# Heads of two mixers made token by token, normed along the free axis, then turned by transposes

## The chip, the cores and the metric

One core of one Trainium2 chip runs the whole program. The time is that of one execution on the device, in microseconds; the median of several executions is taken. The engines are named as in the profile: PE (TensorE), DVE (VectorE), ACT (ScalarE), POOL (GpSimd), SP (SyncE, which issues the transfers).

## What is computed

Two layers of an encoder trunk on 512 tokens of width 1024, all in fp32. The change lies in the first half of a layer, the mixer, where the outputs of eight heads of 128 channels are normed over their channels:

```python
def rms_norm(x, g):
    xf = x.astype(jnp.float32)
    y = xf * lax.rsqrt(jnp.mean(xf * xf, axis=-1, keepdims=True) + EPS)
    return (y * g.astype(jnp.float32)).astype(x.dtype)
...
    o = o.transpose(1, 0, 3, 2, 4).reshape(b, s, DA_HEADS, DA_V_DIM)
    o = rms_norm(o, out_g) * (1.0 - lam_init)
...
    o = rms_norm(o, out_g) * jax.nn.silu(g)
    return o.reshape(b, s, HG_WIDTH)
...
        x = x + jnp.concatenate([y_a, y_b.astype(y_a.dtype)], axis=-1) @ w_out[l]
        x = x + conv_glu_ffn(rms_norm(x, ffn_norm_g[l]), w_up[l], conv_w[l], conv_b[l], w_down[l])
```

The first norm is that of the four heads of differential attention (`dao` below), the second that of the four heads of a gated recurrence (`hgo`). Queries and keys of the attention (`dq`, `dk`) have a norm over 64 channels and a rotation of their own.

## The kernel before

**Tiles.** Activations lie transposed: 128 channels on the partitions, the 512 tokens along the free axis. A weight unit is 128 by 1024 values; for a product of fp32 accuracy it is split in a high and a low part (`wH`, `wL`), and each product is three matmuls of 512 columns (`triple`, L506 to L508). SP loads a unit, ACT makes the high part (`high_now`, L805), POOL the low part (`split`, L440, or `split_whole`, L446), and each has two buffers.

**Slots.** A layer's mixer is 40 slots. Slots 0 to 31 multiply one unit of `w_in` each (24 matmuls), slots 32 to 39 one of `w_out`. Between and behind the two halves of a slot's unit, each engine does its part of the recurrence (`item`, slots 7 to 30), of the attention (`scores`, `turn`, `values`, `row_max`, `combine`, `exponentials`, `back`, slots 17 to 33) and of the norms. There is no scheduler: each engine's order is the order of the code in its own loop over the slots, and an engine that waits holds up all that stands behind it on that engine.

**Norms of heads.** `STATS` says in which slot a norm's squares are summed: dq and dk in the slots 13, 14, 18, 19, 21, 22, 25, 26; the heads hgo0 in 20, hgo1 in 23, dao0 in 24, dao1 in 27, dao2 in 30, hgo2 in 31, hgo3 in 32, dao3 in 34. In such a slot ACT squares the head (`stat_square`), PE multiplies the squares with a constant matrix (`stat`, L546), which sums over the partitions and puts the sum in all of them; in the next slot ACT takes logarithm and exponential of 128x512 (`fin`, L839, L842) and DVE multiplies (`norm`, L1201; `rope` for dq and dk). For dao3 all of it is in slot 34. Then a hgo head is multiplied with its gate (`gating`, L1208), and each head is split in high and low (`high_out` on ACT, L939, `low_out` on DVE, L1215) for the product with `w_out`: heads 0 and 1 of `OUT_HEADS` in slot 31, 2 and 3 in slot 32, 4 and 5 in slot 33, 6 and 7 in slot 34, each pair wanted by PE one slot later.

**Bank 6.** One bank of PSUM takes turns: tokens of `hi` and `dv` (`to_tokens`), the attention's weights turned by four transposes (`turn`, L650), and the sums of `stat`. The order is a list (`bank6_uses`), and each use waits until ACT has read the one before.

Of the kernel before, what the change touches and what calls it, by code (L numbers as in the profile page):

```python
# [64 lines left out]
FINISH = {31: (0, 1), 32: (2, 3), 33: (4, 5), 34: (6, 7)}  # L65
LATE = 34

# [15 lines left out]
def bank6_uses():  # L83

    uses = []
    for s in range(SLOTS):
        if tokens_of(s) is not None:
            uses.append(("tokens", tokens_of(s)))
        if s == LATE:
            uses.append(("stat", STATS[s]))  # L90
        if step_of(s - 1) is not None:
            uses.append(("turn", step_of(s - 1)))
        if s in STATS and s != LATE:
            uses.append(("stat", STATS[s]))
    return {use: i for i, use in enumerate(uses)}
# [52 lines left out]
def build(nc, xT, wts, cst, msk, par, lbl, pos, outT):  # L148
# [14 lines left out]
    with ctx:  # L163
# [23 lines left out]
        sb("back", [P, 24])  # L187
# [55 lines left out]
        bank6_free = signal("bank6_free", B6)  # L243
        swapped = [signal(f"swapped{c}", 4 * 64) for c in range(2)]
        squared = signal("squared", 16)
        rstd_ln = signal("rstd_ln", 16)
        rstd_ready = signal("rstd_ready", 16)
        scaled = signal("scaled", 16)
        hg_q = signal("hg_q", 18)
# [17 lines left out]
        od_ready = signal("od_ready", HEADS)  # L267
# [111 lines left out]
        with nc.Block() as block:  # L379
# [122 lines left out]
            def _(pe):  # L502
                for l in range(DEPTH):
# [38 lines left out]
                    def stat(job):  # L542
# [3 lines left out]
                        pe.matmul(bank[6][:], cst_at(C_MEAN_H if job[0] in ("dk", "dq") else C_MEAN_D), sq[:, JOB[job] % 2, :],  # L546
                                  start=True, stop=True).then_inc(bank6_full.sem, 1)
# [70 lines left out]
                    def gather(pair):  # L618

                        pe.wait_ge(*hg_q.at(l, 9 * pair + 9))  # L620
                        for r in range(2):
                            hd = 2 * pair + r
                            pe.wait_ge(*st_ready.at(l, 4 * pair + 2 + r + 1))
                            for i in range(TT):
                                o = bank[2 + r][:, i * P:i * P + P]
                                pe.matmul(o, HI[:, i, hd * P:hd * P + P], A[:, r, i, :], start=True, stop=False)
                                if i > 0:
                                    m = pe.matmul(o, ST[:, r, 0, i - 1, :], head(QQ, 1, hd, i, 1), start=False, stop=i == TT - 1)
                                if i < TT - 1:
                                    m = pe.matmul(o, ST[:, r, 1, TT - 2 - i, :], head(QQ, 0, hd, i, 1), start=False, stop=True)  # L630
# [22 lines left out]
                    def values(a):  # L653
# [4 lines left out]
                        for k in range(TT):  # L658
                            m = pe.matmul(bank[7][:, qt * P:qt * P + P], V[:, k, hd * P:hd * P + P], wT[:, a % 2, k, :],  # L659
# [23 lines left out]
                    def out_half(u, half):  # L683
# [18 lines left out]
                        else:  # L702
                            if half == 0 and j < 6:
                                pe.wait_ge(*exps.at(l, STEPS))
                            elif half == 0:
                                pe.wait_ge(*((od_ready.at(l, HEADS)) if j == 6 else bank6_free.at(l, B6)))
# [8 lines left out]
                    for s in range(SLOTS):  # L715
# [8 lines left out]
                        if s == LATE:  # L724
                            stat(STATS[s])
# [6 lines left out]
                        if s in STATS and s != LATE:  # L732
                            stat(STATS[s])
                        if n is not None and n % PAIR_ITEMS == CARRY:
# [55 lines left out]
            def _(act):  # L790
# [7 lines left out]
                for l in range(DEPTH):  # L798
# [32 lines left out]
                    def fin(job):  # L831


                        j = JOB[job]
# [665 lines left out]
```

## Time and profile before

| | |
|---|---|
| median of three runs | 1429.94 us (1429.18 to 1429.96) |
| the profiled execution | 1427.0 us |
| its span | 1425.2 us |
| PE busy | 1388.1 us, 97% of the span |
| DVE, ACT, POOL busy | 846.8, 616.0, 711.5 us |
| chain that ended last | PE 78%, issue 7%, POOL 6%, DVE 4%, ACT 4% |
| POOL's split of a unit in one piece (L446) | 2412 ns |
| ACT's high part of a unit (L805) | 1057 ns |
| granted clock of PE | 0.997 of full speed |

A row of a timeline gives start and length in us, engine, line, operation, output and inputs, and in brackets how long the engine stood idle before it and what released it. A matmul's row is longer than the time that it holds up the next one, since matmuls overlap: the distance of two starts is the price.

### The profile page before, as it was taken

To read this page: it belongs to the slowest core of one execution; us is meant where nothing else is said; L and a number is where in the kernel's file an instruction comes from. 1 tells how busy PE (TensorE), PEld (TensorE's weight loads), DVE (VectorE), ACT (ScalarE), POOL (GpSimd) and SP (SyncE) were. 2 spreads that over 40 slices of the span, in tenths; PEclk is the share of its full clock that TensorE was granted. 3 is DMA by queue.
4 is the path that set the end of the run, shared out by engine and by line. 5 is a ranking of instruction groups with operands and counts; after the bars stand their busy time and mean duration, and the time that the engine had idled before them with its cause. 6 is when DMAs were issued, how large, how long until landed. Compare 5 with 4: busy or idle time off the path is not lost.

```text
span 1425.2 us, 18904 instructions
## 1 busy us (share of the span) xinstructions
PE 1388.1 (97%) x6556; PEld 1122.3 (79%) x6556; DVE 846.8 (59%) x1091; ACT 616.0 (43%) x878; POOL 711.5 (50%) x543
## 2 busy tenths in 40 slices
PE   5999999999999999999999999999999999999999
PEld 4887877777788888888878778777777888888887
DVE  6666698555676677600267767975557776675001
ACT  6343455374444444422343435554745444443211
POOL 2596376336444444444577853753374444444443
PEclk9999999999999999999999999999999999999999
DMA  4212122112232232223222221121132232232223
GB/s 152 89 60 92 57 60 75 60 45 89 89 103 88 88 103 91 101 92 103 88 89 75 67 91 52 58 74 45 61 103 76 101 101 90 88 103 94 98 98 108
DMA packets 36822, 121.07 MB, mean 85 GB/s; under 512 B 4897, under 2 KB 5409, under 8 KB 36769
## 3 DMA queue, kind: packets, MB, share of 16 engines
q1 hardware_dynamic: 36480, 119.64, 25.3%
q8 instruction: 33, 0.54, 0.2%
q10 hardware_dynamic: 288, 0.72, 0.1%
q14 instruction: 21, 0.16, 0.0%
HBM read 114.05 MB, written 2.10 MB: 81 GB/s over the span
## 4 chain that ended last, share of the span: by engine, by line
PE 78%; issue 7%; POOL 6%; DVE 4%; ACT 4%; DMA 0%; SPq 0%; POOLq 0%; DVEq 0%; ACTq 0%
PE bank L506 22%; PE bank L508 21%; PE bank L507 21%; PE bank L583 3%; POOL wL L446 3%; PE bank L641 2%; PE bank L659 2%; PE bank L546 2%; POOL rstd L370 1%; POOL wL L440 1%; ACT wH L805 1%; PE bank L650 1%; DVE QQ L1274 1%; DVE hL L358 1%; PE bank L614 1%
## 5 line engine op out<-in xcount | busy, mean ns | idle before, releaser
L446 POOL TENSOR_TENSOR wL<-raw,wH 128x1024 fp32r<-128x1024 f32 x142 | 342.6, 2412 | 419.7 <-ACT wH L813 357.3
L506 PE MATMUL bank<-hH,wH 128*128 128x512 f32 x1216 | 487.2, 401 | 25.4 <-POOL wL L440 11.7
L508 PE MATMUL bank<-hL,wH 128*128 128x512 f32 x1216 | 475.6, 391 | 0.0
L507 PE MATMUL bank<-hH,wL 128*128 128x512 f32 x1216 | 475.1, 391 | 0.0
L440 POOL TENSOR_TENSOR wL<-raw,wH 128x256 fp32r<-128x256 f32 x272 | 250.5, 952 | 196.3 <-ACT wH L805 196.3
L506 PEld LDWEIGHTS bank<-hH,wH 128*128 128x128 f32 x1216 | 229.2, 188 | 97.3 <-issue 40.9
L508 PEld LDWEIGHTS bank<-hL,wH 128*128 128x128 f32 x1216 | 229.1, 188 | 49.6
L507 PEld LDWEIGHTS bank<-hH,wL 128*128 128x128 f32 x1216 | 229.5, 189 | 44.9 <-issue 0.5
L813 ACT ACTIVATE wH<-raw 128x1024 fp32r<-128x1024 f32 x116 | 122.5, 1056 | 182.5 <-PE bank L508 179.8
L805 ACT ACTIVATE wH<-raw 128x1024 fp32r<-128x1024 f32 x95 | 100.4, 1057 | 150.0 <-PE bank L508 149.3
L506 PE MATMUL bank<-gH,wH 128*128 (+1 forms) x352 | 137.3, 390 | 0.2 <-issue 0.2
L507 PE MATMUL bank<-gH,wL 128*128 (+1 forms) x352 | 137.0, 389 | 0.0
L508 PE MATMUL bank<-gL,wH 128*128 (+1 forms) x352 | 137.0, 389 | 0.0
L1421 DVE TENSOR_TENSOR x<-x,bank 128x512 f32<-128x512 f32 x16 | 10.9, 683 | 199.8 <-PE bank L508 199.8
L1388 DVE TENSOR_TENSOR uu<-bank,rms 128x512 f32<-128x512 f32 x88 | 60.5, 691 | 92.4 <-PE bank L508 66.7
L1395 DVE SCALAR_TENSOR_TENSOR ua<-uu,cw,ua 128x511 f32<-128x511 f32 x44 | 114.4, 2601 | 1.5
L473 POOL TENSOR_TENSOR KK<-KK,T 128x512 f32<-128x512 f32 x56 | 71.6, 1300 | 30.1 <-PE bank L583 30.1
L506 PEld LDWEIGHTS bank<-gH,wH 128*128 128x128 f32 x352 | 66.1, 188 | 14.9 <-issue 0.9
L508 PEld LDWEIGHTS bank<-gL,wH 128*128 128x128 f32 x352 | 66.1, 188 | 13.8
L507 PEld LDWEIGHTS bank<-gH,wL 128*128 128x128 f32 x352 | 66.1, 188 | 13.5
L1031 ACT ACTIVATE ua<-ua 128x512 f32<-128x512 f32 x44 | 27.9, 633 | 94.2 <-DVE ua L1395 94.2
L1274 DVE TENSOR_TENSOR QQ<-QQ,T 128x512 f32<-128x512 f32 x56 | 66.7, 1230 | 0.0
(161 smaller groups left out, 1734.5 us busy)
## 6 DMA issues: line engine op xcount, KB each, us to landing
raw<-wts SPq DMA_DIRECT2D x211, 512.0 KB, 3.2
x<-xT SPq DMA_DIRECT2D x8, 256.0 KB, 5.5
swp<-K SPq DMA_DIRECT2D x32, 64.0 KB, 2.0
swp<-QO SPq DMA_DIRECT2D x32, 64.0 KB, 2.6
outT<-x SPq DMA_DIRECT2D x8, 256.0 KB, 2.0
raw<-wts ACTq DMA_DIRECT2D x1, 512.0 KB, 3.8
W<-pos SPq DMA_DIRECT2D x1, 256.0 KB, 6.9
R<-par SPq DMA_DIRECT2D x2, 109.0 KB, 3.4
```

The costliest lines, as they stand in the source:

```text
L440: m = pool.tensor_tensor(wL[:, s, at], raw[:, s, at], wH[:, s, at].bitcast(F32), ALU.subtract)
L446: pool.tensor_tensor(wL[:, s, :], raw[:, s, :], wH[:, s, :].bitcast(F32), ALU.subtract)\
L473: last = pool.tensor_tensor(v, v, w.to_broadcast([P, n, h]), ALU.mult)
L506: pe.matmul(out, wH[:, s, a:a + P], rhs_h, start=first, stop=False)
L507: pe.matmul(out, wL[:, s, a:a + P], rhs_h, start=False, stop=False)
L508: return pe.matmul(out, wH[:, s, a:a + P], rhs_l, start=False, stop=last)
L583: m = pe.matmul(o.rearrange("p (n two h) -> p n two h", two=2, h=h), kx[:, r, i * P:i * P + P], crossing(QQ, hd, i, h, 0), start=True, sto ...
L805: act.activation(wH[:, u % 2, :], raw[:, u % 2, :], ACT.Copy).then_inc(w_high.sem, 1)
L813: act.activation(wH[:, s, :], raw[:, s, :], ACT.Copy).then_inc(w_high.sem, 1)
L1274: last = dve.tensor_tensor(v, v, w[:, :, 1 - half, :].to_broadcast([P, S // h, h]), ALU.mult)
L1388: dve.tensor_tensor(uu[:, q, c, :], bank[2 * q + c][:], rms[:], ALU.mult).then_inc(up_ev.sem, 1)
L1395: dve.scalar_tensor_tensor(dst[:, q, 0:S - 1], uu[:, q, c, 1:S], w(2), dst[:, q, 0:S - 1], ALU.mult, ALU.add).then_inc(conv_done.sem, 1)
```

## The change

The products that make a head (`gather` for hgo, `values` for dao) swap their two operands, so that a head comes out with tokens on the partitions and channels along the free axis. ACT squares it as before. `stat` is gone for heads: DVE sums the squares along the free axis (`add_up`), ACT's `fin` works on 128x4, DVE's `norm` multiplies each token's row, four transposes on PE turn the head into bank 6 (`to_columns`), and ACT copies it out with the gain (`columns_out`). The transposes of a head stand at the end of the slot after the one in which its squares are taken, those of dao3 at the end of slot 34. For dao3, high and low part are made out of bank 6, in slot 35.

```diff
-FINISH = {31: (0, 1), 32: (2, 3), 33: (4, 5), 34: (6, 7)}
+FINISH = {31: (0, 1), 32: (2, 3), 33: (4, 5), 34: (6,), 35: (7,)}
...
+SCALED = {s if s == LATE else s + 1: job for s, job in STATS.items() if job[0] in OF_HEADS}
...
+                    def to_columns(job):
+
+                        pe.wait_ge(*scaled.at(l, JOB[job] + 1))
+                        bank6(("heads", job))
+                        for i in range(TT):
+                            m = pe.transpose(bank[6][:, i * P:i * P + P], out_head(*job)[:, i * P:i * P + P], cst_at(C_IDENT))
+                        m.then_inc(bank6_full.sem, 1)
...
-                                pe.matmul(o, HI[:, i, hd * P:hd * P + P], A[:, r, i, :], start=True, stop=False)
+                                pe.matmul(o, A[:, r, i, :], HI[:, i, hd * P:hd * P + P], start=True, stop=False)
...
-                            m = pe.matmul(bank[7][:, qt * P:qt * P + P], V[:, k, hd * P:hd * P + P], wT[:, a % 2, k, :],
+                            m = pe.matmul(bank[7][:, qt * P:qt * P + P], wT[:, a % 2, k, :], V[:, k, hd * P:hd * P + P],
...
-                        if s in STATS and s != LATE:
+                        if s in STATS and STATS[s][0] not in OF_HEADS:
                             stat(STATS[s])
+                        if s in SCALED:
+                            to_columns(SCALED[s])
...
+                        if job[0] in OF_HEADS:
+                            r = root_of[:, j % 2, :]
+                            act.wait_ge(*summed.at(l, TURNED[job] + 1))
+                            act.activation(r, sums[:, j % 2, :], ACT.Ln, bias=eps, scale=1.0 / P).then_inc(rstd_ln.sem, 1)
+                            act.wait_ge(*rstd_ln.at(l, TURNED[job] + 1))
+                            act.activation(r, r, ACT.Exp, scale=-0.5).then_inc(rstd_ready.sem, 1)
+                            return
...
+                    def columns_out(job):
...
+                        act.wait_ge(*bank6_full.at(l, BANK6[("heads", job)] + 1))
+                        gain = R[:, R_HGG:R_HGG + 1] if kind == "hgo" else dag[:, 0:1]
+                        act.activation(out_head(kind, hd), bank[6][:], ACT.Identity, scale=gain).then_inc(bank6_free.sem, 1)
...
+                        if OUT_HEADS[p] == LAST_HEAD:
+                            act.wait_ge(*bank6_full.at(l, BANK6[("heads", LAST_HEAD)] + 1))
+                            act.activation(yH[:, p, :], bank[6][:], ACT.Identity, scale=dag[:, 0:1]).then_inc(yH_ready.sem, 1)
+                            return
...
                         if s - 1 in STATS and s - 1 != LATE:
                             fin(STATS[s - 1])
+                        if s - 1 in SCALED and s - 1 != LATE:
+                            columns_out(SCALED[s - 1])
...
+                    def add_up(job):
+
+                        j = JOB[job]
+                        dve.wait_ge(*squared.at(l, j + 1))
+                        dve.tensor_reduce(sums[:, j % 2, :], sq[:, j % 2, :].rearrange("p (i c) -> p i c", i=TT), axis=AX.X, op=ALU.add)\
+                           .then_inc(summed.sem, 1)
...
-                        dve.scalar_tensor_tensor(o, o, gain, rstd[:, j % 2, :], ALU.mult, ALU.mult).then_inc(scaled.sem, 1)
+                        rows = root_of[:, j % 2, :].rearrange("p (i o) -> p i o", o=1).to_broadcast([P, TT, P])
+                        dve.tensor_tensor(o.rearrange("p (i c) -> p i c", i=TT), of.rearrange("p (i c) -> p i c", i=TT), rows, ALU.mult)\
+                           .then_inc(scaled.sem, 1)
...
                             row_max(step_of(s))
+                        if s in SCALED and s != LATE:
+                            norm(SCALED[s])
                         if n is not None:
                             grow(pair, lv)
```

In short: `summed` counts the sums, `fin` no longer reads bank 6 for a head, and `gating` and `high_out` wait for `columns_out` instead of the norm.

PE at the end of slot 21 (C is the identity or the constant matrix, QQ a hgo head, W and wT the attention's weights), before:

```order
L508 MATMUL bank<-hL,wH 128x512
L546 MATMUL bank<-sq,C 128x512 [waits bank6_free,squared]
L659 MATMUL bank<-wT,V 128x128 [waits bank6_free]
L659 MATMUL bank<-wT,V 128x128 x3
L583 MATMUL bank<-QQ,kx 128x128 [waits a_msk,kx_ready,hg_q]
```

and in the changed kernel:

```order
L553 MATMUL bank<-sq,C 128x512 [waits bank6_free,squared]
L561 MATMUL bank<-C,QQ 128x128 [waits bank6_free,scaled]
L561 MATMUL bank<-C,QQ 128x128 x3
L674 MATMUL bank<-V,wT 128x128 [waits bank6_free]
L674 MATMUL bank<-V,wT 128x128 x3
L598 MATMUL bank<-QQ,kx 128x128 [waits a_msk,kx_ready,hg_q]
```

The transposes of hgo0 stand directly behind the `stat` of dk2, which uses the same bank; slot 25 has the same pair with dao0 and dk3.

ACT in slots 32 and 33 (ACT_TABLE_LOAD and T belong to the gates' silu, yH is the high part of a head), before:

```order
L805 ACTIVATE wH<-raw 128x1024 [waits w_used,raw_in1]
L839 ACTIVATE rstd<-bank,C 128x512 [waits scaled,bank6_full]
L842 ACTIVATE rstd<-rstd 128x512 [waits bank6_free]
L859 ACTIVATE sq<-QQ 128x512 [waits oh_ready]
L939 ACTIVATE yH<-QO 128x512 [waits scaled]
L939 ACTIVATE yH<-QQ 128x512 [waits gated]
L916 ACTIVATE wT<-bank 128x512 [waits pv_mm,bank6_full]
```

and in the changed kernel:

```order
L820 ACTIVATE wH<-raw 128x1024 [waits w_used,raw_in1]
L855 ACTIVATE root_of<-sums,C 128x4 [waits summed,scaled]
L857 ACTIVATE root_of<-root_of 128x4 [waits rstd_ln]
L888 ACTIVATE QO<-bank,dag 128x512 [waits bank6_full]
L880 ACTIVATE sq<-QQ 128x512 [waits oh_ready]
L972 ACTIVATE yH<-QO 128x512 [waits bank6_free]
L972 ACTIVATE yH<-QQ 128x512 [waits gated]
L945 ACTIVATE wT<-bank 128x512 [waits pv_mm,bank6_full]
```

Two activations of 512 columns have become two of 4 columns and one of 512 that waits for PE's transposes and frees bank 6.

DVE in slot 21 (E and sm are the attention's, A the recurrence's), before:

```order
L1311 TENSOR_REDUCE sm<-bank 128x1 [waits sc_mm]
L1311 TENSOR_REDUCE sm<-bank 128x1
L1274 TENSOR_TENSOR QQ<-QQ,T 128x256x2 [waits tot_ready,hg_q,lv_mm]
L1274 TENSOR_TENSOR QQ<-QQ,T 128x256x2
L1201 SCALAR_TENSOR_TENSOR QQ<-QQ,R,rstd 128x512 [waits rstd_ready]
L1171 TENSOR_TENSOR QO<-bank,rms 128x512 [waits w_used]
```

and in the changed kernel:

```order
L1357 TENSOR_REDUCE sm<-bank 128x1 [waits sc_mm]
L1357 TENSOR_REDUCE sm<-bank 128x1
L1242 TENSOR_TENSOR QQ<-QQ,root_of 128x512 [waits rstd_ready]
L1320 TENSOR_TENSOR QQ<-QQ,T 128x256x2 [waits tot_ready,hg_q,lv_mm]
L1320 TENSOR_TENSOR QQ<-QQ,T 128x256x2
L1207 TENSOR_TENSOR QO<-bank,rms 128x512 [waits w_used]
```

The norm has moved ahead of `grow`; the sum along the free axis stands at the end of the slot before.

## Rows read from the trace of the kernel before

**Rows 1.** Page, part 1: busy us, share of span, instructions.

```profile
PE 1388.1 (97%) x6556; PEld 1122.3 (79%) x6556; DVE 846.8 (59%) x1091; ACT 616.0 (43%) x878; POOL 711.5 (50%) x543
```

**Rows 2.** Waits of PE, 130 to 350 us: us, times, longest.

```profile
PE bank L650 <- ACT rstd L839: 0.7, 1, 0.7
PE bank L506 <- POOL wL L446: 0.6, 2, 0.4
```

**Rows 3.** Timeline of PE, slots 22 to 27 of layer 0: start, length.

```profile
199.11 0.60 PE L650 MATMUL bank<-C,W 128*128 128x128 f32 x4
...
199.78 0.40 PE L507 MATMUL bank<-hH,wL 128*128 128x512 f32 x1
...
202.32 1.02 PE L546 MATMUL bank<-sq,C 128*128 128x512 f32 x2
203.18 1.05 PE L659 MATMUL bank<-wT,V 128*128 128x128 f32 x8
...
236.24 1.05 PE L659 MATMUL bank<-wT,V 128*128 128x128 f32 x8
...
247.89 0.82 PE L599 MATMUL bank<-C,KK 128*128 128x128 f32 x6
248.64 1.13 PE L641 MATMUL bank<-K,QO 64*128 64x512 f32 x4
```

**Rows 4.** Timeline of PE, slot 21 of layer 0.

```profile
188.37 0.60 PE L650 MATMUL bank<-C,W 128*128 128x128 f32 x4
...
191.56 1.02 PE L546 MATMUL bank<-sq,C 128*128 128x512 f32 x2
```

**Rows 5.** Timeline of ACT, end of slot 21, starts of 22 and 26.

```profile
190.51 0.68 ACT L924 ACTIVATE E<-bank,sm 128x512 f32<-128x512 f32 x1
...
191.84 1.06 ACT L805 ACTIVATE wH<-raw 128x1024 fp32r<-128x1024 f32 x1
192.78 0.69 ACT L839 ACTIVATE rstd<-bank,C 128x512 f32<-128x512 f32 x1
...
236.60 0.67 ACT L839 ACTIVATE rstd<-bank,C 128x512 f32<-128x512 f32 x1
```

**Rows 6.** Timeline of DVE, slot 21 and slot 28.

```profile
185.54 0.98 DVE L1322 SCALAR_TENSOR_TENSOR W<-E,sm 128x512 f32<-128x512 f32 x1
...
190.65 1.23 DVE L1201 SCALAR_TENSOR_TENSOR QQ<-QQ,R,rstd 128x512 f32<-128x512 f32 x1
...
261.04 0.74 DVE L1201 SCALAR_TENSOR_TENSOR QO<-QO,dag,rstd 128x512 f32<-128x512 f32 x1
```

**Rows 7.** Timeline of ACT, slots 31 to 33.

```profile
295.92 0.60 ACT L916 ACTIVATE wT<-bank 128x512 f32<-128x512 f32 x1 [2.29 <-PE bank L650]
...
305.39 0.62 ACT L939 ACTIVATE yH<-QQ 128x512 fp32r<-128x512 f32 x1
...
312.05 0.67 ACT L839 ACTIVATE rstd<-bank,C 128x512 f32<-128x512 f32 x1
```

**Rows 8.** Timeline of PE, slot 33 of layer 0, then of layer 1.

```profile
312.77 0.65 PE L650 MATMUL bank<-C,W 128*128 128x128 f32 x4 [0.67 <-ACT rstd L839]
...
316.02 1.05 PE L659 MATMUL bank<-wT,V 128*128 128x128 f32 x8
...
1017.53 0.66 PE L650 MATMUL bank<-C,W 128*128 128x128 f32 x4 [0.67 <-ACT rstd L839]
```

**Rows 9.** Groups by line and form: busy us, mean ns, idle before.

```profile
L1311 DVE TENSOR_REDUCE sm<-bank 128x1 f32<-128x512 f32 x64 | 41.1, 683 | 10.1 <-PE bank L641 9.9
...
L650 PE MATMUL bank<-C,W 128*128 128x128 f32 x128 | 19.2, 272 | 1.3 <-ACT rstd L839 1.3
...
L971 ACT ACTIVATE sm<-sm 128x16 f32<-128x16 f32 x1 | 0.2, 198 | 0.0
```

**Rows 10.** Timeline of DVE, slot 32 of layer 0.

```profile
302.71 0.68 DVE L1208 TENSOR_TENSOR QQ<-QQ,T 128x512 f32<-128x512 f32 x1
...
305.52 1.14 DVE L1215 TENSOR_TENSOR yL<-QO,yH 128x512 fp32r<-128x512 f32 x1 [2.13 <-ACT yH L939]
```

More of the change, by code:

```diff
@@ L64 @@
 OUT_HEADS = [("dao", 0), ("dao", 1), ("dao", 2), ("hgo", 0), ("hgo", 1), ("hgo", 2), ("hgo", 3), ("dao", 3)]
-FINISH = {31: (0, 1), 32: (2, 3), 33: (4, 5), 34: (6, 7)}
+FINISH = {31: (0, 1), 32: (2, 3), 33: (4, 5), 34: (6,), 35: (7,)}
 LATE = 34
+OF_HEADS = ("hgo", "dao")
+LAST_HEAD = ("dao", HEADS - 1)
+SCALED = {s if s == LATE else s + 1: job for s, job in STATS.items() if job[0] in OF_HEADS}
+TURNED = {job: j for j, job in enumerate(SCALED.values())}
 def item_of(s):
@@ L186, in build @@
         R = sb("R", [P, NR])
-        sb("back", [P, 24])
+        sums = sb("sums", [P, 2, TT])
+        root_of = sb("root_of", [P, 2, TT])
+        sb("back", [P, 8])
         bank = [ctx.enter_context(nc.psum_tensor(f"bank{i}", [P, S], F32)) for i in range(8)]
@@ L545, in stat @@
                         bank6(("stat", job))
-                        pe.matmul(bank[6][:], cst_at(C_MEAN_H if job[0] in ("dk", "dq") else C_MEAN_D), sq[:, JOB[job] % 2, :],
-                                  start=True, stop=True).then_inc(bank6_full.sem, 1)
+                        pe.matmul(bank[6][:], cst_at(C_MEAN_H), sq[:, JOB[job] % 2, :], start=True, stop=True)\
+                          .then_inc(bank6_full.sem, 1)
+                    def to_columns(job):
[4 more added lines that the diff above has]
+                        m.then_inc(bank6_full.sem, 1)
                     def item(n):
@@ L1357, in _ @@
                             prep(s // 18)
+                        if s == LATE:
+                            add_up(STATS[s])
+                            norm(STATS[s])
                         for p in FINISH.get(s, ()):
-                            if s != LATE or p < KT - 1:
-                                low_out(p)
-                        job = STATS[LATE] if s == LATE else STATS.get(s - 1) if s - 1 != LATE else None
-                        if job in ROPES:
-                            rope(ROPES.index(job))
-                        elif job is not None:
-                            norm(job)
-                        if s == LATE:
-                            low_out(KT - 1)
+                            low_out(p)
+                        if STATS.get(s - 1) in ROPES:
+                            rope(ROPES.index(STATS[s - 1]))
+                        if s in STATS and s != LATE and STATS[s][0] in OF_HEADS:
+                            add_up(STATS[s])
                         if l == 0 and s in (2, 4, 5):
```

55 lines of the change are left out of this document (28 added, 27 removed).

## Prediction

> **What bounds the kernel now.** I read the page first: PE is busy 97% of the span, of the other engines DVE comes next with 59% [rows 1]. Then the waits of PE in the mixer stage of layer 0, where every line of the change lies: in 220 us PE waits 1.3 us in all, 0.7 of it before the transposes of `turn` in slot 33 [rows 2]. So an instruction added to PE or taken from it counts in full, except where PE already waits, and a new wait on PE counts in full. Then PE's timeline for prices, and the timelines of ACT and DVE for when things are ready. Layer 1 repeats layer 0's pattern (its idle time at slot 33 is the same 0.67 us [rows 8]), so I work out layer 0 and double.
>
> **What PE is rid of.** Per layer eight `stat` matmuls for the heads. One starts at 202.32 and the next instruction at 203.18 [rows 3]: 0.86 us. 8 x 0.86 = 6.88 us off.
>
> **What PE gets.** Per layer eight groups of four transposes (`to_columns`). No such group stands in the trace for heads, but `turn` is the same operation, 128x128 f32 against the identity. It starts at 199.11, and the second matmul behind it at 199.78, 0.67 later; two matmuls of the stream are 0.23 apart with no transposes ahead, so four transposes cost 0.44. Ahead of other f32 matmuls there are six transposes from 247.89 to 248.64, 0.125 each, which makes 0.50 for four [rows 3]. Most of the new groups stand before `values`, some before a stream. The bounds are 0.41 and 0.50; I take 0.43, nearest to the row with four: 8 x 0.43 = 3.44 us on.
>
> One transpose alone has a duration of 272 ns [rows 9], but the four of a group lie over one another and are over in 0.60 us [rows 3]. Were they in series, a group would take 4 x 0.272 = 1.09, dearer than the `stat` that it replaces; that is a rival below. The Trainium skill (TensorE: Matmul & The Clock Gate, "Part 4: PE-mode transpose") gives about 275 ns for a 128x128 transpose inside a kernel and says nothing of how a group overlaps; whoever prices a group by it gets 1.10 us. The trace agrees on the one and speaks against the sum.
>
> **Operands swapped.** `gather` and `values` change which side is stationary. Both sides are 128x128 f32 and the counts are equal: nothing, between -0.3 and +0.3 us per layer.
>
> **Two new waits on PE.** `to_columns` of a head stands one slot behind the place of its `stat`. In slots 21 and 25 that place also holds the `stat` of a rope job (dk2, dk3), which stays. Both use bank 6, so the transposes wait until ACT has read the `stat` result. ACT gets to that (L839) only after the high half of a weight unit (L805, 1.06 us), which itself waits for the same slot's last matmul. Slot 25: PE is free at 236.24 [rows 3], ACT's L839 starts at 236.60 and takes 0.67 [rows 5], so bank 6 is free at 237.27, and PE goes on some 0.05 later, as it does in slot 33 (312.05 + 0.67 = 312.72 against 312.77) [rows 7, 8]. The wait is 1.08 us. Slot 21: PE's `stat` starts at 191.56, ends its share at 192.42 by the 0.86 above [rows 4]; L839 runs from 192.78 to 193.47 [rows 5]: 1.1 us. But PE now reaches this point 0.86 earlier, and ACT is late there already: its last exponential starts at 190.51 and two of them with the reads take 1.45, so L805 follows at 191.84 without a gap [rows 5]. ACT's inputs in that slot come from PE as well, and most of ACT moves along; the part that hangs on DVE does not. I take 1.23. Behind the waiting transposes stand `values`, the next level of the recurrence and the next scores; all are delayed with it and nothing hides it, since PE is the bound. Together 2.31 us on, between 1.8 and 3.3.
>
> **DVE.** Per head it gets a sum along the free axis. The nearest row is the row maximum, 683 ns from PSUM [rows 9]; the norm by columns takes the place of one by a full tile, which took 0.74 to 1.23 us [rows 6]. So about 0.65 more per head. DVE is 59% busy, but in slots 20 to 22 it runs behind PE without idle time. There W of slot 21 is done at 185.54 + 0.98 = 186.52 and PE's transposes of it start at 188.37: 1.85 us of cover [rows 4, 6]. PE comes 0.86 earlier, DVE 0.65 later, which leaves 0.34. I count nothing. If the sum costs 1.23 (the dear duration of the norm row, as with POOL busy beside it), 0.24 us of wait appears and ACT's exponentials slip by up to 0.5, so up to 0.75 per layer. The norm now stands ahead of `grow` and the gating; `grow`'s result is first wanted when PE enters slot 22, after the new wait above, and is ready by then.
>
> **ACT in the slots 31 to 33.** Here ACT sets the time: it runs through from the copy at 295.92 (the last at which it waits for PE) to 312.72, where it frees bank 6 and PE, idle for 0.67, starts `turn` [rows 7, 8]. Whatever PE saves behind 295.92 and ahead of 312.77 is lost in this wait. That is two exchanges of a `stat` for four transposes (the ends of slots 31 and 32): 2 x 0.43 = 0.86 us given back. ACT's own work: `fin` on 128x4 instead of 128x512. A small activation (128x16) takes 198 ns [rows 9], two with the pass from one to the other some 0.45 (an estimate) against 1.24 (L839 and L842 as they follow each other). For it comes the copy out of bank 6 with a gain, 0.67 long by L839, which also reads bank 6 with an operand per partition [rows 5], 0.6 to the next start. Slot 32: 0.45 + 0.6 against 1.24, 0.2 earlier. But DVE now does the norm of hgo2 (which waits for this `fin`) ahead of the gating of hgo0, and ACT's L939 at 305.39 waits for that gating. Today it is done at 302.71 + 0.68 [rows 10]; now it comes after about 303.5 + 1.1 + 0.7 to 1.1, for POOL's split runs beside it and a tensor-tensor there took 1.14 [rows 10], so 305.3 to 305.8: ACT between 0.2 earlier and 0.4 late. Slot 33: `fin` plus the copy, 1.05 to its end, against the 0.67 of L839 alone: 0.35 later. In sum ACT frees bank 6 between 0.1 and 0.75 later; I take 0.5.
>
> **Slots 33 to 35, the last head.** Four transposes more at the end of slot 33, and in slot 34 a `stat` gone and four transposes come: counted above. `values` of the last step starts at 316.02 [rows 8] and ends 1.05 later; from there square, sum, two small activations, norm: about 3.5 us, and PE is in slot 34 for 24 matmuls of 0.23, 5.5 us. The transposes then do not wait. Behind them ACT and DVE split the head (0.7 + 0.7 us and the passes) under the 12 matmuls of slot 35's first half, 2.7 us: cover left 0.5 to 1 us. ACT's weight unit for slot 36 comes about 1 us later than now, with POOL's 2.4 us behind it, and is still 1 us early. I count nothing.
>
> **Sum per layer:** -6.88 + 3.44 + 2.31 + 0.86 + 0.50 = +0.23 us. Both layers: +0.5 us. The profiled execution took 1427.0 us, so 1427.5; the median of the runs shown is 2.9 higher at 1429.94, so I forecast **1430.4 us**. With all low ends (transposes 0.41, waits 1.8, ACT 0.1, operands -0.3) it is -1.1 per layer, 1427.7; with all high ends (0.50, 3.3, DVE's 0.24, ACT 0.75, +0.3) +2.6 per layer, 1435.1, which needs them all at once.
>
> **Rivals.**
> - *The new waits are short* (faster): the gain of 3.44 per layer stands, and slots 21 and 25 cost nearly nothing, because ACT frees bank 6 by the time `stat` is over. -3.44 + 0.86 + 0.5 = -2.1 per layer, 1425.7. Against it: ACT's weight copy can't start before the slot's last matmul and lies ahead of L839 in both slots [rows 5]. For it: only that nothing in the trace shows a group in this place. 0.11, with all mixtures that gain over 2.9 us.
> - *DVE's lag becomes PE's wait* (slower): the extra sum and the earlier norm push W, row maxima and exponentials of slots 20 to 24 past the point at which PE wants them. It decides once DVE slips more than 1.0 us per head there (1.85 less 0.86). At 1.2 us a head, with `fin` waiting for the sum, PE would wait in four slots for 0.3 to 0.5 each, +1.5 per layer on my sum: 1433.4. For it: DVE has no idle time in these slots. Against it: its idle time returns by slot 24. 0.08.
> - *Transposes in series* (slower): each of a group waits for the one before, as they might with other waits around them: 1.09 instead of 0.43 [rows 9]. 8 x 0.66 = 5.3 per layer on my sum, less some 0.9 that slot 33's idle time hides, 4.4: 1439. Against it: 0.60 for four [rows 3]. 0.02. The skill's page named above leads to the same time.
>
> **How the numbers follow.** The forecast's case has 0.79. What a measurement can tell from no change is 0.2%, 2.9 us: 1427.1 to 1432.8. The first rival lies below it, the other two above: 0.11, 0.79, 0.10. The range takes in the sum's ends as far as single ones reach and stops short of the rivals: 1427.6 to 1432.8.
>
> **What would show it.** In the profile after: PE busy about 3.4 us less per layer, and PE's waits up by about as much. Transposes of heads in slots 21 and 25 preceded by 1.0 to 1.3 us of idle time put down to ACT's L839, none at the other six heads. `turn` in slot 33 preceded by about 2 us of idle time, not 0.67. DVE rows of the sum near 0.65 us. The prediction is wrong if the heads' transposes cost more than 0.5 us a group, if PE waits for DVE anywhere in slots 20 to 24, or if idle time before the slot 21 and 25 groups is under half a microsecond.

## Result and the profile after

The changed kernel takes **1436.14 us** (median of 5 runs, 1434.73 to 1436.60); the kernel before takes 1429.31 beside it (5 runs, 1428.99 to 1429.96). The ratio of the means is 1.0044, 95% interval 1.0033 to 1.0055: slower by 0.44%. The forecast was 1430.4 with a range up to 1432.8. The profiled execution took 1434.73 us, span 1432.5. One of e8's eleven executions below was slow, 2319.67 us at a mean granted clock of 0.557, and is in no ratio; e8's median without it is 1425.16.

The page's part 1 of the kernel after, in the form of [rows 1]:

```profile
PE 1385.2 (97%) x6588; PEld 1122.8 (78%) x6588; DVE 860.5 (60%) x1107; ACT 612.4 (43%) x890; POOL 716.2 (50%) x543
```

PE's busy time falls by 2.9 us in two layers, less than the forecast 3.4 a layer, but this row can't be read as the saving. The row of a 128x512 matmul is 0.39 us long where the next one starts 0.23 later, so busy stretches overlap, and a wait that is new leaves such a tail uncovered. The saving is read from starts, below.

The waits of PE from 130 to 350 us of the kernel after (us, times, longest), where [rows 2] had two lines:

```profile
PE bank L561 <- ACT rstd L861: 2.2, 2, 1.2
PE bank L665 <- ACT QQ L888: 1.8, 1, 1.8
PE bank L665 <- DVE W L1368: 1.2, 1, 1.2
PE bank L561 <- ACT wT L945: 0.5, 1, 0.5
...
PE bank L665 <- ACT QO L888: 0.3, 1, 0.3
```

L561 is `to_columns`, L665 is `turn`. The first two lines were forecast (two bank-6 meetings, and a wait of about 2 us in slot 33). The lines on DVE's W, on ACT's wT and on ACT's QO were not. Where each stands is in PE's timeline of layer 0 (start, length, last the idle time and what ended it), the answer to [rows 3, 4, 8]:

```profile
190.67 0.63 PE L665 MATMUL bank<-C,W 128*128 128x128 f32 x4 [1.19 <-DVE W L1368]
...
193.90 1.02 PE L553 MATMUL bank<-sq,C 128*128 128x512 f32 x2
196.11 0.63 PE L561 MATMUL bank<-C,QQ 128*128 128x128 f32 x4 [1.19 <-ACT rstd L861]
196.57 1.06 PE L674 MATMUL bank<-V,wT 128*128 128x128 f32 x8
...
240.32 0.63 PE L561 MATMUL bank<-C,QO 128*128 128x128 f32 x4 [1.02 <-ACT rstd L861]
240.78 1.06 PE L674 MATMUL bank<-V,wT 128*128 128x128 f32 x8
...
301.78 0.60 PE L561 MATMUL bank<-C,QO 128*128 128x128 f32 x4
302.22 1.06 PE L674 MATMUL bank<-V,wT 128*128 128x128 f32 x8
...
307.55 0.66 PE L665 MATMUL bank<-C,W 128*128 128x128 f32 x4 [0.27 <-ACT QO L888]
...
316.86 0.66 PE L665 MATMUL bank<-C,W 128*128 128x128 f32 x4 [1.78 <-ACT QQ L888]
...
320.74 0.63 PE L561 MATMUL bank<-C,QQ 128*128 128x128 f32 x4 [0.47 <-ACT wT L945]
321.21 1.06 PE L674 MATMUL bank<-V,wT 128*128 128x128 f32 x8
```

**How far PE is behind, slot by slot.** I compare starts of the same instruction group in both traces. The transposes of W in slot 18, ahead of every norm of a head, start at 154.71 before and 156.33 after: +1.62 that has nothing to do with the edit (below, b1). Take that off, and PE's lag at `values` is: slot 20 -0.85, slot 21 +2.53, slot 24 +1.26, slot 25 +2.92, slot 31 +1.25, slot 33 +3.57 (321.21 against 316.02 [rows 8]), and +3.16 behind slot 34. Layer 1 gives +3.54 up to slot 33. The sum on record gives +0.66 up to slot 33 and +0.23 behind slot 34. So a layer lost 2.9 us more than forecast, two layers 5.9 us, which is the whole miss of 5.7 between the medians and the forecast.

The prices of the operations come out of the groups by line and form (busy us, mean ns, idle before), in the form of [rows 9]:

```profile
L1231 DVE TENSOR_REDUCE sums<-sq 128x4 f32<-128x512 f32 x16 | 10.8, 676 | 0.0
...
L1242 DVE TENSOR_TENSOR QQ<-QQ,root_of 128x512 f32<-128x512 f32 x8 | 6.7, 834 | 8.2 <-ACT root_of L857 8.2
...
L888 ACT ACTIVATE QQ<-bank,R 128x512 f32<-128x512 f32 x8 | 5.4, 676 | 0.3
```

The sum costs 0.68 (0.60 to the next start) and the copy out of bank 6 0.68. They are as priced, and so are the transposes: a group of four at 301.78 is followed by the next instruction at 302.22, 0.44 later.

### The profile page after: what moved, and what is told of

It reads as the page before. It is cut to its first block, busy times and chain, and to the rows that moved or that the text cites. A ratio compares the mean times of both kernels' runs of the same rounds, so it can differ in the third digit from the quotient of the medians.

```text
span 1432.5 us, 18994 instructions
## 1 busy us (share of the span) xinstructions
PE 1385.2 (97%) x6588; PEld 1122.8 (78%) x6588; DVE 860.5 (60%) x1107; ACT 612.4 (43%) x890; POOL 716.2 (50%) x543
## 4 chain that ended last, share of the span: by engine, by line
PE 78%; issue 6%; DVE 6%; POOL 5%; ACT 4%; DMA 0%; SPq 0%; POOLq 0%; DVEq 0%; ACTq 0%
PE bank L513 22%; PE bank L515 22%; PE bank L514 22%; PE bank L598 3%; POOL wL L453 2%; PE bank L656 2%; PE bank L674 2%; POOL rstd L377 1%; POOL wL L447 1%; DVE QQ L1320 1%; ACT wH L820 1%; DVE hL L365 1%; PE bank L629 1%; PE bank L665 1%; PE bank L553 1%
## 5 line engine op out<-in xcount | busy, mean ns | idle before, releaser
L447 POOL TENSOR_TENSOR wL<-raw,wH 128x256 fp32r<-128x256 f32 x272 | 255.1, 968 | 191.0 <-ACT wH L820 191.0
```

Of the source, the lines that this page charges most:

```text
L447: m = pool.tensor_tensor(wL[:, s, at], raw[:, s, at], wH[:, s, at].bitcast(F32), ALU.subtract)
```

## Experiments

All times stand beside runs of the kernel before on the same chip. "Lag per layer" is the shift against the first trace of the kernel before, from the first transposes of W (slot 18) to `values` of slot 33; both layers agree within 0.04 us in every kernel, and a repeat of the kernel before gives 0.00.

| kernel | median us (runs) | before | ratio of means, 95% interval | lag per layer, us |
|---|---|---|---|---|
| changed | 1436.14 (5) | 1429.31 | 1.0044, 1.0033 to 1.0055 | +3.57 |
| e1 columns apart | 1431.73 (11) | 1429.67 | 1.0010, 1.0001 to 1.0019 | +0.93 |
| e2 gating first | 1432.63 (10) | 1429.67 | 1.0018, 1.0009 to 1.0028 | +2.30 |
| e3 head 0 later | 1433.38 (11) | 1429.67 | 1.0021, 1.0012 to 1.0030 | +1.50 |
| e4 all three | 1424.89 (5) | 1429.67 | 0.9965, 0.9951 to 0.9978 | -0.99 |
| e5 before, one sum | 1429.23 (10) | 1429.15 | 0.9999, 0.9990 to 1.0009 | 0.00 |
| e6 before, two sums | 1431.91 (10) | 1429.15 | 1.0017, 1.0008 to 1.0027 | +0.87 |
| e7 columns first | 1425.15 (7) | 1429.15 | 0.9974, 0.9963 to 0.9985 | -0.89 |
| e8 turned W first | 1425.33 (11) | 1429.59 | 0.9973, 0.9964 to 0.9982 | -2.33 |
| e9 products ahead | 1435.12 (5) | 1429.59 | 1.0041, 1.0027 to 1.0054 | +3.51 |
| e10 best of all | 1424.28 (5) | 1429.59 | 0.9964, 0.9950 to 0.9977 | -3.06 |

The lag is free of one thing that the medians hold: each fall of PE's granted clock costs an execution 1.53 us (below, b1). The executions of the kernel before had a mean granted clock of 0.995 to 0.996, e4's 0.997 to 0.998, e7's 0.996 to 0.997, and all of e8's but the one named above 0.994 to 0.996. So differences of 1 to 2 us between medians can be the clock's; the argument goes by the lags.

### e1: the meetings on bank 6

```diff
+MOVED = {21: 23, 25: 27}
+COLUMNS = {MOVED.get(s, s): job for s, job in SCALED.items()}
...
-                        if s in SCALED:
-                            to_columns(SCALED[s])
+                        if s in COLUMNS:
+                            to_columns(COLUMNS[s])
```

(The order of uses of bank 6 and ACT's `columns_out` follow `COLUMNS` too.)

> The transposes of the recurrent head 0 go from slot 21 to 23 and those of the differential head 0 from slot 25 to 27, slots where no square product of a dk or dq stands right ahead of them; the norms stay where they are, so DVE's order is untouched. Theory 'three places': the changed kernel's saving is eaten by two meetings on bank 6 (1.19 and 1.02 us of idle time a layer), by DVE's lag in slot 21 (1.19) and by slots 31 to 33. Then the two ACT waits ahead of the transposes go (2.2 a layer), the wait of the turn in slot 21 for DVE stays at about 1.2, and the time is 1436.1 - 4.4 = 1431.7 (1431 to 1432.5). Rival 'DVE sets slots 21 to 25': the idle time only moves to the next turn, and the time stays within 1 us of 1436.1. Rival 'it is the start': 1.6 us of the loss lies ahead of slot 14 and comes again in every kernel that is built from the changed one.

Measured: 1431.73, the expected time. PE's waits, 130 to 350 us:

```profile
PE bank L667 <- ACT QQ L890: 1.8, 1, 1.8
PE bank L667 <- DVE W L1370: 1.2, 1, 1.2
...
PE bank L563 <- ACT wT L947: 0.5, 1, 0.5
PE bank L667 <- ACT QO L890: 0.3, 1, 0.3
```

The 2.2 us line is gone and the others haven't moved. A layer is 2.64 us shorter for 2.21 us of idle time: these waits of PE cost some 0.2 us each more than their rows say. The rival of a DVE that sets slots 21 to 25 falls: the wait for DVE stayed at one place and one size.

### e2: the gating ahead of the norm

```diff
+                        for p in FINISH.get(s, ()):
+                            if OUT_HEADS[p][0] == "hgo" and p != 5:
+                                gating(OUT_HEADS[p][1])
                         if s in SCALED and s != LATE:
                             norm(SCALED[s])
...
-                            if OUT_HEADS[p][0] == "hgo":
+                            if p == 5:
                                 gating(OUT_HEADS[p][1])
```

> DVE's gating of the recurrent heads 0, 1 and 3 goes ahead of the norm in the same slot; only head 2's stays behind it. Theory 'three places': in slot 33 the norm of head 3 waited 2.8 us for its root while the gating that ACT's copy and then ACT's copy of the turned W (and so bank 6) wait for stood behind it. With head 1's product ahead of the norm the wait of the last transposes in slot 33 for ACT (0.47 us) goes and the turn's wait there (1.78) may shrink: 0.5 to 1.0 us a layer, 1434.1 to 1435.1. Rival 'ACT sets slots 31 to 33 by its own work': the gating is early but ACT no earlier, within 0.4 us of 1436.1.

Measured: 1432.63, and 1.27 us a layer less than the changed kernel, more than expected. The changed kernel's DVE and then ACT in slot 33 show the chain that the edit cuts:

```profile
312.73 0.75 DVE L1368 SCALAR_TENSOR_TENSOR W<-E,sm 128x512 f32<-128x512 f32 x1
316.27 0.89 DVE L1242 TENSOR_TENSOR QQ<-QQ,root_of 128x512 f32<-128x512 f32 x1 [2.79 <-ACT root_of L857]
317.08 2.37 DVE L1250 TENSOR_TENSOR QQ<-QQ,T 128x512 f32<-128x512 f32 x2
```

```profile
318.33 0.63 ACT L972 ACTIVATE yH<-QQ 128x512 fp32r<-128x512 f32 x1 [1.52 <-DVE QQ L1250]
319.48 0.63 ACT L972 ACTIVATE yH<-QQ 128x512 fp32r<-128x512 f32 x1 [0.52 <-DVE QQ L1250]
320.02 0.58 ACT L945 ACTIVATE wT<-bank 128x512 f32<-128x512 f32 x1
```

DVE idles 2.79 us for the root of head 3. Behind the norm stand two gating products, ACT's two roundings wait for those (1.52 and 0.52), and behind the roundings stands ACT's copy of the turned W, the one that empties bank 6 for PE's last transposes. With the gating first, PE's 0.47 us wait is gone, and the turn's wait in slot 33 is 1.17 in place of 1.78.

### e3: slots 20 and 21 without a head

```diff
-STATS = {13: ("dk", 0), 14: ("dq", 0), 18: ("dk", 1), 19: ("dq", 1), 20: ("hgo", 0), 21: ("dk", 2), 22: ("dq", 2),
-         23: ("hgo", 1), 24: ("dao", 0), 25: ("dk", 3), 26: ("dq", 3), 27: ("dao", 1), 30: ("dao", 2),
+STATS = {13: ("dk", 0), 14: ("dq", 0), 18: ("dk", 1), 19: ("dq", 1), 21: ("dk", 2), 22: ("dq", 2),
+         23: ("hgo", 0), 24: ("dao", 0), 25: ("dk", 3), 26: ("dq", 3), 27: ("dao", 1), 28: ("hgo", 1), 30: ("dao", 2),
```

> The recurrent head 0 is squared, summed and scaled in slots 23 and 24 (in place of head 1's) and head 1 in slots 28 and 29; slots 20 and 21 have no head's work any more. Theory 'three places': both waits of slot 21 go, the turn's for DVE (1.19) and the transposes' for ACT (1.19), and with them DVE's slow small operations beside GpSimd; slot 25 keeps its 1.0. 2.4 us a layer, 1436.1 - 4.8 = 1431.3 (1430.5 to 1432.5). Rival 'only the bank': DVE's wait comes back in slots 21 to 24 in another place, and 1.2 a layer is gained, 1433.7. Rival 'the DVE lag is not the sum's': the turn in slot 21 waits for DVE as before by 1 us or more, although no sum stands ahead of it.

Measured: 1433.38, above the expected 1430.5 to 1432.5, and 2.07 us a layer less than the changed kernel. The transposes' wait in slot 21 is gone, but the one for DVE is only halved (0.54 us), though no sum stands ahead of it. DVE and then POOL in slot 21 of this kernel:

```profile
186.35 0.57 DVE L1364 TENSOR_TENSOR sm<-sm,lamc 128x1 f32<-128x1 f32 x1
186.95 1.51 DVE L1365 TENSOR_SCALAR E<-E,sm 128x512 f32<-128x512 f32 x1
188.50 1.68 DVE L1368 SCALAR_TENSOR_TENSOR W<-E,sm 128x512 f32<-128x512 f32 x1
```

```profile
185.72 1.19 POOL L474 TENSOR_TENSOR T<-T 128x256 f32<-128x256 f32 x2 [2.86 <-PE bank L598]
186.86 2.78 POOL L480 TENSOR_TENSOR KK<-KK,T 128x512 f32<-128x512 f32 x2
```

In the kernel before the same three DVE operations took 0.16, 0.92 and 0.98 us (W's row is in [rows 6]). DVE, then POOL of that stretch in the kernel before:

```profile
184.39 0.16 DVE L1318 TENSOR_TENSOR sm<-sm,lamc 128x1 f32<-128x1 f32 x1
184.59 0.92 DVE L1319 TENSOR_SCALAR E<-E,sm 128x512 f32<-128x512 f32 x1
```

```profile
184.61 1.37 POOL L467 TENSOR_TENSOR T<-T 128x256 f32<-128x256 f32 x2 [3.71 <-PE bank L583]
185.94 3.04 POOL L473 TENSOR_TENSOR KK<-KK,T 128x512 f32<-128x512 f32 x2
```

In e3 the first of the three ends at 186.92, where GpSimd's T is done (186.91). E ends at 188.46 and W at 190.18, 0.2 and 0.5 us behind the ends of KK's two products, which lie near 188.25 and at 189.64. GpSimd starts when PE's `item` ends. PE now comes 0.86 us earlier to it, since no `stat` stands at the end of slot 20, while DVE comes as before, so GpSimd's KK products stand beside DVE's E and W rather than its short T products.

The Trainium skill (SBUF — State Buffer, "Who interferes with whom") says that a DVE operation with two inputs in SBUF and a GpSimd operation that reads SBUF exclude each other, the later one standing still until the first is done. The end of the first agrees with that. W's agrees but for 0.2 us: it ends 0.5 behind KK, where its whole 0.75 (its length at 312.73, under e2) would be expected. The price of standing beside KK is W's 1.68 against the 0.98 of the kernel before. No run takes GpSimd's products out of the slot, so the exclusion is read from these ends and not tested by itself.

### e5 and e6: the cover measured in the kernel before

```diff
+                        if s == 20:
+                            for i in range(N):
+                                dve.tensor_reduce(spare[:, 4 * i:4 * i + 4],
+                                    cosT[:].rearrange("p (i c) -> p i c", i=TT), axis=AX.X, op=ALU.add)
```

Each sum is of 128x512, at the end of slot 20. N is 1 in e5 and 2 in e6. Nothing reads the sums.

> The kernel before, with one more sum of 128x512 along the free axis on DVE at the end of slot 20, of a table that nobody waits for; PE's work is untouched. W of slot 21 was done 1.85 us ahead of PE's transposes. Theory 'GpSimd doubles the lag': a DVE that is 0.6 later runs its two products under GpSimd's KK products, at 1.0 to 1.7 us each in place of 0.92 and 0.98; W ends 1.1 to 1.6 later, so that 0.3 to 0.7 of cover is left and PE doesn't wait. Rival 'plain cover': W ends 0.6 later, 1.25 left. Both: the time within 1 us of 1429.7.

> The same with two such sums, 1.2 us. Rival 'plain cover': 1.85 - 1.2 = 0.65 left, no wait of PE for W in slot 21, the time as before. Theory 'GpSimd doubles the lag': W ends 2.4 to 3.2 later, PE waits 0.5 to 1.3 us for it in slot 21, once a layer, +1.0 to +2.6 on the whole: 1430.7 to 1432.3.

Measured: e5 as before; e6 PE waits, once a layer, and a layer is 0.87 us longer. DVE in slot 21 of e6, then PE:

```profile
184.65 1.27 DVE L1368 TENSOR_REDUCE back<-cosT 128x4 f32<-128x512 f32 x2
...
186.62 0.24 DVE L1318 TENSOR_TENSOR sm<-sm,lamc 128x1 f32<-128x1 f32 x1
186.90 1.49 DVE L1319 TENSOR_SCALAR E<-E,sm 128x512 f32<-128x512 f32 x1
188.43 1.68 DVE L1322 SCALAR_TENSOR_TENSOR W<-E,sm 128x512 f32<-128x512 f32 x1
```

```profile
190.25 0.63 PE L650 MATMUL bank<-C,W 128*128 128x128 f32 x4 [0.67 <-DVE W L1322]
```

Plain cover would have left 1.85 - 1.19 = 0.66 us. The two sums cost 2.54: 1.19 themselves and 1.35 by which the three operations behind them ran longer. In e5 one sum cost 0.60 + 0.68 (0.26, 0.80 and 1.68 us in place of 0.16, 0.92 and 0.98), so 0.59 is left. The time of e6 is 2.8 us above before's, of which 1.7 is this; the rest may be the clock, which its trace shows fallen in both layers (below, b1).

The same account closes for every kernel of the slot. It says where the cover went; the reason for the longer operations is the one under e3. In it "sum ahead" counts 0.60 for each sum and -0.60 for W made ahead of the eviction, and "left" is the time by which W was done ahead of PE's arrival (worked out from starts and lengths as above):

| kernel | PE earlier | sum ahead | three operations longer | 1.85 less these | left, measured |
|---|---|---|---|---|---|
| before, one sum (e5) | 0 | 0.60 | 0.68 | +0.57 | +0.59 |
| before, two sums (e6) | 0 | 1.19 | 1.35 | -0.69 | -0.69 |
| head 0 later (e3) | 0.86 | 0 | 1.70 | -0.71 | -0.71 |
| changed | 0.86 | 0.60 | 1.79 | -1.40 | -1.39 |
| products ahead (e9) | 0.86 | 0 | 1.70 | -0.71 | -0.71 |
| best of all (e10) | 0.86 | -0.60 | 1.00 | +0.59 | +0.58 |

### e9: the four operations for W ahead of the eviction

```diff
+                        if s == 21:
+                            combine(step_of(s - 1))
                         if 0 < s <= N_IN:
                             evict(s - 1)
...
-                        if step_of(s - 1) is not None:
+                        if step_of(s - 1) is not None and s != 21:
                             combine(step_of(s - 1))
```

> The changed kernel with one edit: in slot 21 DVE makes W (combine) ahead of the eviction of the unit's bank, so its four operations for W start 0.6 us earlier, about where they stood before the change. Theory 'GpSimd doubles the lag': the sum's 0.60 us is undone, and so is most of the 1.8 us by which these operations ran longer beside GpSimd's products: PE's wait for W in slot 21 goes from 1.19 us to 0 to 0.3, and 0.9 to 1.5 us a layer come out: 1436.1 - 2.4 = 1433.7 (1433 to 1434.5). Rival 'plain lag': only the 0.6 us is undone, the wait is 0.6: 1434.9. Rival 'the bank takes it': the square product at the slot's end comes earlier but ACT's square, behind the later eviction, does not, and PE waits there or before the transposes for what it gained: 1436.

Measured: 1435.12, above the expected 1433 to 1434.5; lag per layer 3.51 against 3.57. "GpSimd doubles the lag" is too strong here: starting 0.6 us earlier did not bring the operations out from beside KK (1.70 longer, as in e3), so only the sum was undone and the wait for W is 0.54, as "plain lag" has it. And even that was lost, as the third theory has it. PE's timeline of slot 21 in e9:

```profile
188.54 0.63 PE L665 MATMUL bank<-C,W 128*128 128x128 f32 x4 [0.54 <-DVE W L1368]
...
194.60 0.63 PE L561 MATMUL bank<-C,QQ 128*128 128x128 f32 x4 [1.83 <-ACT rstd L861]
```

ACT reads bank 6 (L861) behind its exponentials of the slot, and these wait for DVE's row maxima, which stand behind W and the eviction. In e9 W is earlier and the eviction later, so the row maxima, and with them the emptying of bank 6, come no earlier: 0.54 + 1.83 is 2.37 against 1.19 + 1.19 = 2.38. ACT's row in the changed kernel shows this wait, which the kernel before doesn't have [rows 5]:

```profile
192.99 0.69 ACT L953 ACTIVATE E<-bank,sm 128x512 f32<-128x512 f32 x1 [1.06 <-DVE sm L1357]
```

With the transposes in the slot of a `stat`, the two waits of slot 21 hang on one chain of DVE and ACT.

### e4, e7, e8, e10: taking the waits out together

e4 is e2 and e3 with the transposes of the differential head 0 in slot 27.

> All of it: head 0's work in slots 23 and 24, head 1's in 28 and 29, the transposes of the differential head 0 in slot 27, and the gating ahead of the norm. Theory 'three places': no new wait is left up to slot 31, and PE's whole saving of 3.4 us a layer comes out but for what the slots 31 to 33 swallow: 1436.1 - 2 x (1.2 + 1.2 + 1.0 + 0.5) = 1428.3 (1427 to 1430), no slower than before. Rival 'ACT swallows it': ACT's own chain from slot 31 sets slot 33, so what PE gains before is waited out there, and the wait of the turn in slot 33 grows from 1.8 towards 4 us; 1431 to 1432. Rival 'it is the start': 1.6 us stays on top of either.

Measured: 1424.89, 4.56 us a layer less than the changed kernel; expected were 3.9. Neither rival holds: the turn's wait in slot 33 is 1.2, not 4. This version beats both kernels. Against the kernel before 1.0 us a layer of it stands in the slots 18 to 33 and 0.4 is the exchange of the last head, 2.8 us in all; of the other 2.0 between the medians one fall of the clock would be 1.5 (e4's trace has none, b1's has one).

e7 adds to e4 the first edit below on ACT (for slots 32 and 33), e8 also puts the copy of the turned W ahead of the roundings in slot 33, e10 adds e9's edit:

```diff
+                        if s > 31 and s - 1 in COLUMNS and s - 1 != LATE:
+                            columns_out(COLUMNS[s - 1])
                         if s:
                             high_now(s + 1)
...
-                        if s - 1 in COLUMNS and s - 1 != LATE:
+                        if s < 32 and s - 1 in COLUMNS and s - 1 != LATE:
                             columns_out(COLUMNS[s - 1])
```

```diff
+                        if s == LATE - 1:
+                            back(step_of(s - 1))
                         for p in FINISH.get(s, ()):
                             if p < KT - 1:
                                 high_out(p)
...
-                        if step_of(s - 1) is not None:
+                        if step_of(s - 1) is not None and s != LATE - 1:
                             back(step_of(s - 1))
```

> The kernel of e4 with ACT's copies of the turned heads in slots 32 and 33 ahead of its rounding of the weights and of the roots. Theory: the 1.2 us wait of the turn in slot 33 is ACT's order, not ACT's load: head 2's transposes are done at the end of slot 32, and the copy that frees bank 6 stands behind a 1.06 us rounding and two small operations that wait for DVE's sum. With the copy first the waits of 0.3 and 1.2 us go: up to 1.5 a layer, 1424.9 - 3.0 = 1421.9 (1421.5 to 1423.5). Rival 'ACT is full there': the rounding comes 0.7 later, then the low part on GpSimd and PE's stream wait for it, or the turn waits for W: no gain, 1424 to 1426.

> The kernel of e7 with ACT's copy of the turned W in slot 33 ahead of its roundings of the heads 4 and 5 to yH. In e7 the turn came 1.0 us a layer earlier, and all of it was waited out at the end of the slot: the last transposes of slot 33 found bank 6 not yet emptied (1.3 us), since the copy stood behind a rounding that waited 1.6 us for DVE's gating, which stood behind the norm, which waited for its root. Theory 'order, not load': with the copy right behind the roots the 1.3 us go and 1.0 to 1.5 us a layer come out: 1425.2 - 2.5 = 1422.7 (1421.7 to 1423.5). Rival 'ACT is full there': the roundings are later by the copy's 0.6, and PE's products of slots 34 and 35, or its stream behind GpSimd's low parts, wait for them: 1424.5 to 1426.

> All edits together (e8 with e9's order in slot 21). Of e4's waits the 0.54 us in slot 21 goes too. Theory: e8's time less 2 x 0.5, 1421.7 (1420.7 to 1423); against the kernel before 7 to 8 us less, which is 8 x 2 x 0.43 = 6.9 us of PE's work plus the wait of 0.67 us that stood in slot 33 in both layers. Rival: a new wait takes the place of the 0.54 us, no faster than e8.

Measured: e7 1425.15, no gain on e4, the time of its rival. The waits of e7:

```profile
PE bank L563 <- ACT wT L947: 1.3, 1, 1.3
...
PE bank L667 <- ACT QQ L890: 0.3, 1, 0.3
```

What the turn no longer waited came back whole at the end of the slot. e8 removes that: the 1.3 us line is gone, the lag goes from -0.89 to -2.33 a layer, so it was order and not load. Behind it 0.4 us appears in slot 34 (e8's PE timeline), so about 1.0 a layer is kept:

```profile
315.22 0.50 PE L515 MATMUL bank<-yH,wH 128*128 128x512 f32 x1 [0.42 <-POOL wL L449]
```

Yet e8's median, 1425.33, is no better than e7's and above the expected 1421.7 to 1423.5. Its clock is lower (0.994 to 0.996 against 0.996 to 0.997; next part). e10 takes away the last wait in slot 21 and has the smallest lag, -3.06 a layer; its time, 1424.28, is above the expected 1420.7 to 1423 and can't be told from e4's by these runs. Eight exchanges of 0.43 make 3.44 us a layer, so in e10 most of PE's saving has come out.

### b1: the kernel before once more

> The kernel before once more, with its trace. Its first profiled run took 1427.0 us against a median of 1429.7, so it was one of the quickest. Theory 'start and clock': an ordinary run differs from it in the first 60 us (the first square product of slot 14 at 114 to 115 us in place of 113.3) and in a stretch of lowered clock behind PE's pause after slot 39, not in the slots between; turns and products of slots 18 to 33 keep their distances within 0.1 us. Rival 'it is in the slots': waits stand in slots 18 to 33 that the first trace doesn't show.

Measured: 1429.14 us, one execution. From slot 18 to 33 all distances are those of the first trace. It is 0.82 us later at slot 18, and 2.1 us later at the end. In the feed-forward part of each layer, 30 us behind the end of slot 39, PE pauses 1.9 us in all kernels. The pause ends with GpSimd's low part of a weight unit; in layer 1 of b1:

```profile
1087.23 0.53 PE L506 MATMUL bank<-hH,wH 128*128 128x512 f32 x1 [1.94 <-POOL wL L446]
```

The clock rows of PE around this pause in layer 1 (window, us, PE busy with instructions, granted clock, DMA share, GB/s), first for the kernel before in b1, then for the changed kernel:

```profile
1086.00:1092.00 6.00, 4.77 (x14) 0.72 0.24 87
...
1088.00:1089.00 1.00, 1.00 (x4) 0.50 0.67 209
...
1091.00:1092.00 1.00, 1.00 (x6) 1.00 0.00 0
```

```profile
1092.00:1098.00 6.00, 4.07 (x18) 1.00 0.28 90
```

Behind the pause the granted clock falls to its lower level (0.50 of full speed, 1.2 GHz) for about 3 us in some executions and stays at 2.4 GHz in others. A fall costs 1.53 us: from the first matmul behind layer 1's pause to the sixtieth after it pass 13.8 us in the four traces without a fall there and 15.33 to 15.36 in the nine with one. e1's trace shows a fall between two slots: it is 1.59 us late at slot 33 of layer 0, 1.2 behind slot 34 by that slot's exchange, and 2.63 late at slot 18 of layer 1. Of the traces it fell in both layers of e1, e3 and e6, in layer 0 of e2, in layer 1 of b1, e5, e7, e8, e9 and e10, and in neither of the first trace before, of the changed kernel and of e4. The other loose part is the start: the transposes of slot 18 come at 154.7 to 156.7, in kernels of both kinds (before 154.71, 155.53; with a spare sum 156.29, 155.75; changed 156.33; from it 154.77 to 156.66). The 1.62 us of the changed kernel's trace lies inside this spread and is no sign of an effect of the change.

## Why the prediction failed, point by point

- **PE's saving, right.** -6.88 + 3.44 per layer: between the waits each exchange moves PE by 0.43, and with the waits ordered away e10 reaches -3.06 a layer.
- **Two new waits, right in place and cause, 0.3 small.** Forecast 1.23 and 1.08 on starts; with its 0.43 of transposes taken off, slot 21 cost 1.42 and slot 25 1.23. e1 shows it: 2.64 a layer for both. In slot 21 the division between this wait and the one for W is by place only: e9 halves the one and the other grows by as much.
- **Transposes in series, refuted:** four take 0.44. **Operands swapped, right:** up to slot 20 the lag is the exchange alone (-0.85).
- **DVE's cover in slot 21, the step that failed: "1.85 us of cover ... which leaves 0.34. I count nothing."** It cost 1.53 on starts (1.19 of idle time). The subtraction took the lengths of DVE's products as fixed. The runs show them fixed only where GpSimd stands as before; both a later DVE and an earlier PE move GpSimd's products onto them, which took 1.79 more in the changed kernel (the table above; e5 and e6 without any gain of PE, e3 without any sum). The bound that I set, a sum of 1.23, bounded the wrong operation. The rival *DVE's lag becomes PE's wait* named the right result, and its point of decision, 1.0 us of slip, was passed at 2.4; but it looked for it in four slots where it stands in one. It is also the sign of being wrong that the prediction gave: PE waits for DVE in slots 20 to 24.
- **ACT in slots 31 to 33, half right.** From `values` of slot 31 to that of slot 33 the forecast was +1.36, measured +2.32. The turn's wait in slot 33 is as forecast (1.78 with 0.27 in slot 32 against about 2.0). The price of the norm ahead of the gating was followed up to ACT's rounding, not to what stands behind it: the copy that empties bank 6 for the last transposes, 0.47 of idle time and 0.2 for the restart; the other 0.3 stands ahead of the turn in slot 33. e2 gives 1.27 a layer back.
- **The last head, right:** behind slot 33 the lag falls by 0.41, the exchange alone.
- **The starting point.** The first trace of before, 1427.0 us, was early at the start and free of any fall of the clock; the changed kernel's median of 1436.14 is compared with medians. Of the 6.8 us between the medians 6.3 are the slots; the other 0.5 would be start and clock, which differ from execution to execution.

In sum the miss per layer: 1.53 (DVE) + 0.34 (bank 6) + 0.96 (slots 31 to 33) = 2.8, of 2.9 read from starts.

## What to carry to other kernels

Cover on DVE is not a difference of two starts when GpSimd works in the same stretch: ask what releases GpSimd and whether the edit moves the two against each other, and price DVE's operations at the length that a trace shows beside it (here E 1.5 us in place of 0.9, W up to 1.7 in place of 1.0, while a sum stayed at 0.68). Where an operation moves ahead of others in an engine's order, follow the queue to its end, through every engine that waits for it, until something frees a resource of the bound engine. A saving on the bound engine in small pieces comes out only if the order of the others is laid anew around it: the same change gave +0.44% as made and -0.35% with three pieces of order moved (0.2% by the starts, the rest with the clock and the start).

## What the hardware did that I had not expected

- A DVE operation on 128x1 f32 took 1.24 us in the changed kernel (0.16 before): DVE, then POOL of that stretch:

```profile
186.61 1.24 DVE L1364 TENSOR_TENSOR sm<-sm,lamc 128x1 f32<-128x1 f32 x1
187.88 1.51 DVE L1365 TENSOR_SCALAR E<-E,sm 128x512 f32<-128x512 f32 x1
189.43 1.10 DVE L1368 SCALAR_TENSOR_TENSOR W<-E,sm 128x512 f32<-128x512 f32 x1
```

```profile
186.53 2.58 POOL L480 TENSOR_TENSOR KK<-KK,T 128x512 f32<-128x512 f32 x2
```

  It started 0.08 behind KK's first product and ended at 187.85, where that product ends (186.53 + 2.58 / 2 = 187.82). The same operation took 0.57 in e3, 0.24 in e6 and 0.16 where GpSimd had not yet begun: its length was what was left of GpSimd's product.
- The sum and the eviction from PSUM kept their 0.68 us beside GpSimd in e9's slot 21; E, which also has only one full input, did not (1.52).
- A wait of PE cost 0.20 to 0.34 us more than its idle row. Of this 0.16 is the tail of the matmul ahead of it, 0.39 long where it would have been overlapped after 0.23; the rest stays open.
- The granted clock fell behind a pause of 1.9 us in some executions and not in others, 1.53 us each; that is most of what e8's order saved over e4's, about 1 us a layer. Which position of the pause brings it on was not found.
